# A streaming encoder step on one core: the four slots of the weights' upper halves begin at four residues modulo 256 bytes instead of one

## The chip, the core and the metric

The kernel runs on one core of a Trainium2 chip. The metric is the device time of one execution, in microseconds (us), lower is better.

## The reference, cut to what matters

Two layers over 320 tokens (256 of a prompt, 64 of a decoding step), model width 2048, all in float32:

```
h = rms_norm(x, g_mix)
aq, ak, av, bq, ... , dfl = split(h @ w_in)          # w_in: 2048 x 4392
o = concat(attention A, B, C, D)                      # four kinds of attention
x = x + o @ w_out                                     # 2048 x 2048
x = x + square(relu(rms_norm(x, g_mlp) @ w_up)) @ w_down   # 2048 x 8192, 8192 x 2048
x = x + (ple @ w_ple) * sigmoid(rms_norm(x, g_ple) @ w_ple_gate)
```

The outputs are the activations and the new rows of the caches.

## The kernel before, in words

**Weights in a ring.** All weights stream from HBM through `ring`, four slots of 1024 float32 in each of 128 partitions (4096 bytes a slot). One slot's fill is a unit, 512 KB; unit n goes to slot n modulo 4. There are 408 units a layer: 108 in a first part (w_in, the small projections of C, and part of w_out) and 300 in the tail (the last quarter of w_out 8, the MLP 256, w_ple 4, w_ple_gate 32). SyncE issues the loads (L464).

**Two halves.** The products keep float32 precision by splitting. ACT writes the upper half of a unit, rounded to the format fp32r, to the slot of the same number in `whi` (L1125 in the first part, L1141 in the tail). POOL subtracts it from the ring and writes the lower half, in four pieces of 256 columns: in the first part into the ring itself under the name `rlo` (L655), in the tail into `wlo` (L669). TensorE then makes three products, lower half of the weights by upper half of the activations, upper by lower, and upper by upper.

**w_in** (`w_in_piece`, L767, L769, L770): the activations (`xw`, `xv`) are stationary, loaded as 128x128 blocks, and the weights move, 256 to 512 columns at a time. For two of the three tiles of tokens there are three products, rlo, whi, whi; for the third two, rlo, whi. These pieces are woven into the attention by hand written lists (`FILL`, `AT`), so that TensorE has work while ACT and DVE do softmax.

**The tail** (`gemm_chunk`, `tail_unit`, `product`; L706, L707, L708): here the weights are stationary and the activations move, 320 columns at a time. A unit is two blocks of 128 rows by 512 columns: for each of 4 column blocks m and 2 row blocks k come wlo with the upper activations (L706), whi with the lower (L707), whi with the upper (L708), 24 matmuls. Four PSUM banks take a chunk of eight units, and the other four are emptied by DVE meanwhile. The MLP is four times 32 units of w_up and 32 of w_down.

**Waits.** TensorE waits for `lo_ready` (POOL's lower half of the unit), POOL for `hi_ready` (ACT), ACT for `raw_loaded` (the DMA) and for `unit_used` (TensorE has done with the unit four before). A load in the tail waits for `lo_ready` of the unit four before.

**Where things lie.** Addresses in SBUF come from `sb`, one after another, or are given. The offset of a partition's byte modulo 256 is called the residue here. Steps from block to block and from slot to slot are multiples of 256 bytes in the tail, so a tile keeps its residue throughout (512 bytes from m to m, 2048 from k to k in the weights, 1280 from block to block in the activations). Residues before:

| operand | role | residue |
|---|---|---|
| `whi`, `wlo`, `ring`, `rlo` | all four slots | 128 |
| `xw`, `xv` | stationary in w_in | 128 |
| `xhi`, `hhi` | moving, upper halves | 128 |
| `xlo` | moving, lower half of w_up and w_ple_gate | 192 |
| `hlo` | moving, lower half of w_down | 64 |
| `pleh`, `plel` | moving, both halves in w_ple | 160 |
| `hlast` | moving, lower half in the last of w_out | 160 |

`ahead` is a scratch tile of 3072 float32 that shares its place with `whi`, used while attention runs.

Of the kernel before, what the change touches and what calls it, by code (L numbers as in the profile page):

```python
# [24 lines left out]
UK = 2  # L25
XW = 256 + 128
RING = 4
# [35 lines left out]
def build(nc, I, O):  # L63
    f32 = mybir.dt.float32
    ALU, ACT, AX = mybir.AluOpType, mybir.ActivationFunctionType, mybir.AxisListType
    X = AX.X
    ctx = ExitStack()
    with ctx:
        f32r = mybir.dt.float32r
        top = [nc.sbuf_base + (-nc.sbuf_base) % 64]  # L70

        def sb(name, shape, dtype=f32, at=None):

            words = 1
            for n in shape[1:]:
                words *= n
            if at is None:
                at = top[0]
                top[0] += 4 * (words + (-words) % 8)
            return nc.alloc_sbuf_tensor_at(name, shape, dtype, offset=at)  # L80

        def sem(name):
            return ctx.enter_context(nc.semaphore(name))

        at = top[0]
# [16 lines left out]
        wlo = sb("wlo", [128, RING, 1024], f32r, top[0] - 4 * RING * 1024)  # L102
        at = top[0]
# [8 lines left out]
        at = top[0]  # L112
        ring = sb("ring", [128, RING, 1024])
        rlo = sb("rlo", [128, RING, 1024], f32r, at)
        at = top[0]
        whi = sb("whi", [128, RING, 1024], f32r)
        ahead = sb("ahead", [128, 3072], at=at)
        table = sb("table", [128, T_END])
        vec = sb("vec", [128, VW])
# [3 lines left out]
        at = top[0]  # L123
# [22 lines left out]
        at = top[0]  # L146
# [41 lines left out]
        hi_ready = sem("hi_ready")  # L188
# [173 lines left out]
        for j in ORDER:  # L362
            PREP_BASE[j] = tuple(_t)
            n = len(PREP[j])
# [320 lines left out]
        def _(pe):  # L685
            mm = nc.tensor.matmul

            def hold(s, value):

                pe.wait_ge(s, value)  # L690
                pe.sem_inc(pe_passed, 1)
# [6 lines left out]
            def tail_unit(l, q4, u):  # L698

                hold(lo_ready, l * HL + N_WU + 4 * q4 + u + 1 - TAIL0)  # L700
                return [w[:, u % RING, :].rearrange("p (a n) -> p a n", a=UK) for w in (whi, wlo)]

            def product(out, w, k, m, x2, start, stop):

# [5 lines left out]
            def gemm_chunk(l, q4, half, chunk_no, src, before_unit=None, before_last=None, units=KB // UK, first=0):  # L710


                nk = UK
                hold(half_free, l * CHUNKS + chunk_no + 1)
                for u in range(units):
                    w = tail_unit(l, q4, first + u)
                    if before_unit:
                        before_unit(u)
                    for m in range(4):
                        if m == 3 and u == 0 and before_last:  # L720
                            before_last()
                        for k in range(nk):
                            last = product(ps[:, 4 * half + m, 0:TOK], w, k, m, src(u * nk + k),
                                           u == 0 and k == 0, u == units - 1 and k == nk - 1)
                        if u == units - 1 and m < 3:
                            last.then_inc(bank_full, 1)
                    last.then_inc(unit_used, 1)
# [264 lines left out]
            with pe.Fori(0, DEPTH) as l:  # L992
# [55 lines left out]
                for c in range(4):  # L1048
                    hold(half_free, l * CHUNKS + 36 + c + 1)
                    w = tail_unit(l, Q_PLE, c)  # L1050
                    for m in range(4):
                        for k in range(2):
                            last = product(ps[:, 4 * (c % 2) + m, 0:TOK], w, k, m, (pleh[:, k, :], plel[:, k, :]),
                                           k == 0, k == 1)
                        last.then_inc(bank_full if m < 3 else unit_used, 1)
# [9 lines left out]
            for i in range(12):  # L1065
# [3 lines left out]
                n = 128 if t < 2 else DSEQ  # L1069
# [45 lines left out]
        def _(act):  # L1115
            A = nc.scalar.activation
# [19 lines left out]
            def upper_halves(l, n, slots=range(RING)):  # L1136

                for s in slots:
                    act.wait_ge(raw_loaded[s], 16 * (l * SLOT + n + 1))
                    act.wait_ge(unit_used, l * UNITS + RING * n + s + 1)  # L1140
                    A(whi[:, s, :], ring[:, s, :], ACT.Copy).then_inc(hi_ready, 1)  # L1141

            def x_uppers(p, b0):

# [86 lines left out]
            def attention(l, j):  # L1231
# [30 lines left out]
                if j == len(GROUPS) - 1:  # L1262
                    upper_halves(l, TAIL0 // RING, (0, 1))
# [6 lines left out]
            with act.Fori(0, DEPTH) as l:  # L1270
# [10 lines left out]
                for j, g in enumerate(GROUPS):  # L1281
# [17 lines left out]
                    attention(l, j)  # L1299

                upper_halves(l, TAIL0 // RING, (2, 3))
                for c in range(4):
                    upper_halves(l, TAIL0 // RING + 1 + c // 2, (2 * (c % 2), 2 * (c % 2) + 1))
                    act.wait_ge(half_free, l * CHUNKS + 2 + c + 1)
                    x_uppers(1, 4 * c)
                    if c < 3:
                        A(hid[:, 4 * c:4 * c + 4, :], x[:, 4 * c:4 * c + 4, :], ACT.Square).then_inc(mlp_squares, 1)
# [576 lines left out]
```

## Time and profile before

| | us |
|---|---|
| median of 3 runs | 3377.69 |
| lowest and highest | 3377.07, 3391.3 |
| the profiled execution's own time | 3379.88 |
| its span | 3378.1 |
| granted TensorE clock over the span | 0.99 |

The profile is of one execution. Busy time is per engine; loads of weights (PEld) run beside matmuls (PE). The tail of the first layer lies at 650 to 1696 us of the span, that of the second at 2316 to 3362. A matmul's duration in the trace goes from its start to its modelled end, and successive ones overlap; the distance between two starts is what each adds.

### The profile page before, as it was taken

The page shows a single profiled execution, that of the slowest core. Times are in us where ns is not written, and L with a number is a line of the kernel's source. Part 1 is how long each engine was busy: PE and PEld are TensorE (multiplying, and loading weights), DVE is VectorE, ACT ScalarE, POOL GpSimd, SP SyncE. Part 2 cuts the span into 40 slices and gives each one's busy share as a digit, 9 for nine tenths or more (in the row PEclk, how much of TensorE's full clock was granted, in tenths as well). Part 3 has the DMA queues.
Part 4 walks back from the last instruction along what each step waited for, and adds up shares of the span by engine and source line. Part 5 has one row for each costly group of instructions (what it writes and reads, how often), then busy time and mean ns, then how long its engine had stood idle before and what let it go on. Part 6 is the DMA issues. An engine that isn't in the chain of part 4 may idle for free.

```text
span 3378.1 us, 60314 instructions
## 1 busy us (share of the span) xinstructions
PE 3285.3 (97%) x20664; PEld 2977.2 (88%) x20664; DVE 1229.2 (36%) x2211; ACT 1138.0 (34%) x1666; POOL 2223.1 (66%) x2989
## 2 busy tenths in 40 slices
PE   7999999999999999999989999999999999999998
PEld 5777766799999999999977776668999999999998
DVE  4334564542041230323253445545411402304143
ACT  3333332433333333334343432424333333333342
POOL 4655200388898898888765551005888988889885
PEclk9999999999999999999999999999999999999999
DMA  5443322354454554544453433224545445455443
GB/s 153 134 123 111 111 73 83 100 152 152 151 151 155 150 152 154 150 154 151 133 157 114 129 93 112 71 84 124 149 151 155 150 151 155 150 152 154 150 145 123
DMA packets 295722, 453.02 MB, mean 134 GB/s; under 512 B 36336, under 2 KB 111344, under 8 KB 294832
## 3 DMA queue, kind: packets, MB, share of 16 engines
q1 hardware_dynamic: 295328, 448.66, 44.0%
q8 instruction: 176, 2.88, 0.3%
q14 instruction: 74, 0.61, 0.1%
q0 software_dynamic: 144, 0.87, 0.1%
HBM read 435.54 MB, written 14.06 MB: 133 GB/s over the span
## 4 chain that ended last, share of the span: by engine, by line
PE 91%; DVE 3%; issue 2%; DMA 1%; ACT 1%; SPq 1%; POOL 0%; DVEq 0%; ACTq 0%; POOLq 0%
PE ps L707 21%; PE ps L708 21%; PE ps L706 20%; PE ps L804 5%; PE ps L792 5%; PE ps L767 5%; PE ps L770 4%; PE ps L769 3%; PE ps L896 2%; DMA ring<-in_w_in 1%; PE ps L931 1%; PE ps L842 1%; PE ps L900 1%; PE ps L899 1%; PE ps L865 1%
## 5 line engine op out<-in xcount | busy, mean ns | idle before, releaser
L669 POOL TENSOR_TENSOR wlo<-ring,whi 128x256 fp32r<-128x256 f32 x2400 | 1803.5, 785 | 786.5 <-ACT whi L1141 786.0
L1141 ACT ACTIVATE whi<-ring 128x1024 fp32r<-128x1024 f32 x600 | 635.9, 1061 | 1350.3 <-PE ps L708 1341.6
L707 PE MATMUL ps<-xlo,whi 128*128 128x320 f32 x2560 | 794.9, 311 | 0.0
L708 PE MATMUL ps<-xhi,whi 128*128 128x320 f32 x2560 | 788.0, 308 | 0.0
L706 PE MATMUL ps<-xhi,wlo 128*128 128x320 f32 x2560 | 781.7, 305 | 0.0
L708 PE MATMUL ps<-hhi,whi 128*128 128x320 f32 x2176 | 672.2, 309 | 0.0
L706 PE MATMUL ps<-hhi,wlo 128*128 128x320 f32 x2176 | 659.3, 303 | 0.0
L655 POOL TENSOR_TENSOR rlo<-ring,whi 128x256 fp32r<-128x256 f32 (+2 forms) x576 | 415.9, 755 | 325.4 <-ACT whi L1125 325.4
L707 PE MATMUL ps<-hlo,whi 128*128 128x320 f32 x2048 | 629.9, 308 | 0.0
L706 PEld LDWEIGHTS ps<-xhi,wlo 128*128 128x128 f32 x2560 | 483.8, 189 | 0.6
L708 PEld LDWEIGHTS ps<-xhi,whi 128*128 128x128 f32 x2560 | 480.6, 188 | 0.0
L707 PEld LDWEIGHTS ps<-xlo,whi 128*128 128x128 f32 x2560 | 480.2, 188 | 0.3
L706 PEld LDWEIGHTS ps<-hhi,wlo 128*128 128x128 f32 x2176 | 408.5, 188 | 0.1
L708 PEld LDWEIGHTS ps<-hhi,whi 128*128 128x128 f32 x2176 | 408.4, 188 | 0.0
L767 PE MATMUL ps<-rlo,xw 128*128 128x512 f32 (+3 forms) x1056 | 366.5, 353 | 32.9 <-DVE xw L1357 16.8
L1347 DVE TENSOR_TENSOR x<-ps,x 128x320 f32<-128x320 f32 x224 | 107.0, 488 | 781.4 <-PE ps L708 764.4
L707 PEld LDWEIGHTS ps<-hlo,whi 128*128 128x128 f32 x2048 | 383.0, 187 | 0.0
L770 PE MATMUL ps<-whi,xw 128*128 128x512 f32 (+3 forms) x1056 | 358.0, 345 | 0.0
L767 PEld LDWEIGHTS ps<-rlo,xw 128*128 128x128 f32 x1056 | 201.4, 191 | 65.3 <-issue 42.5
L1771 DVE SCALAR_TENSOR_TENSOR t<-ps,rfeat 128x320 f32<-128x320 f32 x128 | 61.6, 481 | 517.6 <-PE ps L708 517.4
L769 PE MATMUL ps<-whi,xv 128*128 128x512 f32 (+3 forms) x704 | 243.7, 346 | 0.0
L792 PE MATMUL ps<-hid,ring 128*128 128x320 f32 x768 | 225.3, 445 | 5.7 <-ACT vtok L1189 3.3
(244 smaller groups left out, 3160.7 us busy)
## 6 DMA issues: line engine op xcount, KB each, us to landing
ring<-in_w_up SPq DMA_DIRECT2D x256, 512.0 KB, 3.7
ring<-in_w_down SPq DMA_DIRECT2D x256, 512.0 KB, 3.6
ring<-in_w_in SPq DMA_DIRECT2D x120, 512.0 KB, 3.6
ring<-in_w_out SPq DMA_DIRECT2D x64, 512.0 KB, 4.0
ring<-in_w_ple_gate SPq DMA_DIRECT2D x64, 512.0 KB, 3.6
xsave<-x SPq DMA_DIRECT2D x8, 640.0 KB, 5.9
x<-xsave SPq DMA_DIRECT2D x8, 640.0 KB, 4.3
ring<-in_w_in SPq DMA_DIRECT2D x16, 288.0 KB, 2.9
```

The source lines that it names most:

```text
L655: last = nc.gpsimd.tensor_tensor(rlo[:, s, c:c + w], ring[:, s, c:c + w], whi[:, s, c:c + w].bitcast(f32), ALU.subtract)
L669: last = nc.gpsimd.tensor_tensor(wlo[:, s, c:c + LO_COLS], ring[:, s, c:c + LO_COLS], whi[:, s, c:c + LO_COLS].bitcast(f32), ALU.subtract)
L706: mm(out, lo[:, k, cols], xh, start=start, stop=False)
L707: mm(out, hi[:, k, cols], xl, start=False, stop=False)
L708: return mm(out, hi[:, k, cols], xh, start=False, stop=stop)
L767: mm(out, head, lo[:, k, :], start=(kk == 0), stop=False)
L769: mm(out, xv[:, kk, t * 128:(t + 1) * 128], hi[:, k, :], start=False, stop=False)
L770: last = mm(out, head, hi[:, k, :], start=False, stop=(kk == KB - 1))
L792: last = mm(ps[:, out_bank(r * KB + b), 0:TOK], w[:, k - k0, c:c + 128], hid[:, k, :], start=(k == k0), stop=(k == k1 - 1))
L804: return nc.tensor.transpose(out, in_, ident[0:in_.shape[0], 0:in_.shape[0]])
L1141: A(whi[:, s, :], ring[:, s, :], ACT.Copy).then_inc(hi_ready, 1)
L1347: return V.tensor_tensor(out, a, b, ALU.add)
```

## The change

`whi` gets 1040 columns a slot in place of 1024, of which the first 1024 are used. A slot is then 4160 bytes, so slots 0, 1, 2 and 3 begin at the residues 128, 192, 0 and 64. Nothing else about size or order changes; `table` and all tiles behind it lie 256 bytes further, at the same residues.

```diff
-        whi = sb("whi", [128, RING, 1024], f32r)
+        whi = sb("whi", [128, RING, 1024 + 16], f32r)
+        top[0] = at + 4 * RING * 1024 + 256
         ahead = sb("ahead", [128, 3072], at=at)
@@ tail_unit
-                return [w[:, u % RING, :].rearrange("p (a n) -> p a n", a=UK) for w in (whi, wlo)]
+                return [w[:, u % RING, 0:1024].rearrange("p (a n) -> p a n", a=UK) for w in (whi, wlo)]
@@ upper_halves
-                    A(whi[:, s, :], ring[:, s, :], ACT.Copy).then_inc(hi_ready, 1)
+                    A(whi[:, s, 0:1024], ring[:, s, :], ACT.Copy).then_inc(hi_ready, 1)
```

## Rows read from the trace of the kernel before

**Rows 1.** The page: span, busy time of each engine, granted clock in 40 slices.

```profile
span 3378.1 us, 60314 instructions
...
PE 3285.3 (97%) x20664; PEld 2977.2 (88%) x20664; DVE 1229.2 (36%) x2211; ACT 1138.0 (34%) x1666; POOL 2223.1 (66%) x2989
...
PEclk9999999999999999999999999999999999999999
```

**Rows 2.** The page: the chain that ended last, by engine and by line.

```profile
PE 91%; DVE 3%; issue 2%; DMA 1%; ACT 1%; SPq 1%; POOL 0%; DVEq 0%; ACTq 0%; POOLq 0%
PE ps L707 21%; PE ps L708 21%; PE ps L706 20%; PE ps L804 5%; PE ps L792 5%; PE ps L767 5%; PE ps L770 4%; PE ps L769 3%; PE ps L896 2%; DMA ring<-in_w_in 1%; PE ps L931 1%; PE ps L842 1%; PE ps L900 1%; PE ps L899 1%; PE ps L865 1%
```

**Rows 3.** The page's costliest groups (xcount | busy us, mean ns | idle before).

```profile
L707 PE MATMUL ps<-xlo,whi 128*128 128x320 f32 x2560 | 794.9, 311 | 0.0
L708 PE MATMUL ps<-xhi,whi 128*128 128x320 f32 x2560 | 788.0, 308 | 0.0
L706 PE MATMUL ps<-xhi,wlo 128*128 128x320 f32 x2560 | 781.7, 305 | 0.0
L708 PE MATMUL ps<-hhi,whi 128*128 128x320 f32 x2176 | 672.2, 309 | 0.0
L706 PE MATMUL ps<-hhi,wlo 128*128 128x320 f32 x2176 | 659.3, 303 | 0.0
...
L707 PE MATMUL ps<-hlo,whi 128*128 128x320 f32 x2048 | 629.9, 308 | 0.0
```

**Rows 4.** One line each of w_down, w_up, first w_up (ns min/median/max, first, last start).

```profile
L708 PE MATMUL ps<-hhi,whi x256: 309/309/310, 1014.4 to 1124.9; 128*128 128x320 f32 x128
...
L708 PE MATMUL ps<-xhi,whi x255: 307/307/308, 903.9 to 1013.9; 128*128 128x320 f32 x128
...
L706 PE MATMUL ps<-xhi,wlo x191: 307/308/385, 707.6 to 791.7; 128*128 128x320 f32 x191
```

**Rows 5.** Timeline of w_ple (start us, duration us, engine, line).

```profile
1568.74 0.31 PE L706 MATMUL ps<-pleh,wlo 128*128 128x320 f32 x1
1568.74 0.19 PEld L707 LDWEIGHTS ps<-plel,whi 128*128 128x128 f32 x1
...
1570.94 0.31 PE L706 MATMUL ps<-pleh,wlo 128*128 128x320 f32 x1
```

**Rows 6.** Timeline of PE in w_in, 512 columns.

```profile
44.73 0.39 PE L769 MATMUL ps<-whi,xv 128*128 128x512 f32 x1
...
50.85 0.39 PE L770 MATMUL ps<-whi,xw 128*128 128x512 f32 x1
...
57.36 0.63 PE L770 MATMUL ps<-whi,xw 128*128 128x512 f32 x1
...
59.07 0.63 PE L767 MATMUL ps<-rlo,xw 128*128 128x512 f32 x1
```

**Rows 7.** Windows (PE, PEld, DVE, ACT, POOL busy; granted clock; DMA share, GB/s).

```profile
57.00:59.40 2.40, 2.40 (x7) 1.94 (x6) 0.00 (x0) 2.40 (x4) 2.40 (x4) 0.50 0.00 0
```

**Rows 8.** The tile whi: its instructions (ns min/median/max), what ACT waited for.

```profile
L707 PEld LDWEIGHTS ps<-xlo,whi x2560: 186/187/192, 678.9 to 3361.5; 128*128 128x128 f32 x197
...
L669 POOL TENSOR_TENSOR wlo<-ring,whi x2400: 720/742/1042, 646.4 to 3351.6; 128x256 fp32r<-128x256 f32 x185
...
L770 PE MATMUL ps<-whi,xw x1056: 274/389/632, 35.0 to 2056.6; 128*128 128x512 f32 x96, 128*128 128x256 f32 x48, 128*128 128x264 f32 x16, 128*128 128x288 f32 x16
...
L769 PE MATMUL ps<-whi,xv x704: 274/389/632, 34.6 to 2056.0; 128*128 128x512 f32 x96, 128*128 128x256 f32 x48, 128*128 128x264 f32 x16, 128*128 128x288 f32 x16
L1141 ACT ACTIVATE whi<-ring x600: 1037/1061/1066, 645.1 to 3348.0; 128x1024 fp32r<-128x1024 f32 x150
...
  PE ps L708: 1341.6, 560
```

**Rows 9.** POOL's group in the windows 2600 to 2700 and 2700 to 2800.

```profile
L669 POOL TENSOR_TENSOR wlo<-ring,whi 128x256 fp32r<-128x256 f32 x117 | 93.3, 832 | 7.7 <-ACT whi L1141 7.7
...
L669 POOL TENSOR_TENSOR wlo<-ring,whi 128x256 fp32r<-128x256 f32 x117 | 82.9, 739 | 18.4 <-ACT whi L1141 18.4
```

## The prediction

> **What bounds the kernel now.** I read the page first. TensorE is busy for 97% of the span, almost all of it at the full granted clock [rows 1], and the chain that ended last runs through PE for 91% [rows 2]. Three lines of that chain, L706 to L708, hold 62% of the span: the three products of every 128x128 weight block in the tail of each layer. No other engine is near: POOL 66%, DVE 36%, ACT 34% [rows 1]. So time comes or goes by how often TensorE can start a matmul, and the next view to read is that of the starts. The tail has 14400 matmuls of 320 columns: 2 layers, 300 units, 24 each. The five groups of the page with 2560 or 2176 of them, and that of 2048, hold 14080 [rows 3]; the rest are the first eight units and the four of w_ple.
>
> The page's mean of 303 to 311 ns is no price, because successive matmuls overlap. The price is the distance between starts. 320 columns at 2.4 GHz are 133.3 ns. What the rows show:
> - w_down in the middle of the MLP: the L708 starts of 256 triples run from 1014.4 to 1124.9, so 110.5 / (255 x 3) = **144.4 ns** a matmul. w_up before it: 110.0 / (254 x 3) = 144.4 [rows 4].
> - w_ple: the L706 at 1568.74 and the one at 1570.94 are 15 matmuls apart: **146.7 ns** [rows 5].
> - the first w_up block, after a wait at 707 us: 84.1 / (190 x 3) = **147.5 ns** until its end [rows 4]. Same code, same addresses as the 144.4 of the later w_up.
> - w_in, 512 columns: 28 starts from 44.73 to 50.85, 27 distances, give 226.7 ns against 213.3 ideal, so again 13.3 over. A few us later, from 57.36 to 59.07, four distances take 1.71 us [rows 6] at the granted clock 0.50, 1.2 GHz [rows 7]: 427.5 against 426.7 ideal, no excess at all.
>
> Each matmul thus pays 11 to 14 ns over its columns at 2.4 GHz and nothing at 1.2 GHz. What differs between the stretches is where operands begin modulo 256 bytes. In w_ple the moving operands begin at 160 in all three products, in w_in (512 and 256 columns) everything begins at 128: 13.3 ns over. In w_up they begin at 128, 192, 128, in w_down at 128, 64, 128: 11.1 ns over, that is 3 x 2.2 = 6.7 ns saved in every three. The 147.5 shows that it isn't addresses alone: a stream can also lock into a dearer rhythm and stay in it.
>
> **The change, part by part.** No instruction, wait or DMA is added or removed, and nothing is moved in any queue. The tiles behind whi move by exactly 256 bytes, so their residues stay; the third line (top) gives the same address as the allocation gives by itself. ahead keeps its place and length. What alters is the start of whi in slots 1, 2 and 3.
>
> (a) *whi as the moving operand*, w_in. L769 has 704 matmuls and L770 1056 [rows 8], so there are 704 triples rlo, whi, whi and 352 pairs rlo, whi. rlo stays at 128. In three slots of four the moving start now changes twice in a triple, just as in w_up. By that rhythm a triple saves 6.7 ns and a pair two thirds of it: (704 x 6.7 + 352 x 4.4) x 3/4 = 4.7 us. PE is the chain here too for most of the stage, so I count all of it. Bounds: 0 if changing starts pay only with 320 columns, and all the excess gone, 2816 matmuls x 13.3 x 3/4 = 28 us; on the other side the dearer rhythm of 0.8 ns more, 2 us lost. I take 4.7, the row nearest in form.
>
> (b) *whi as the stationary operand*, the tail. The load of the next weights starts with each matmul: L707's load at 1568.74, at the same time as the L706 matmul [rows 5]. Two reads of SBUF therefore run side by side, and the excess exists only at the clock at which they run fastest. No row has weights at another residue than 128, so this can't be read off. From both sides: w_ple, 160 against 128 throughout, costs the same 13.3 as w_in with 128 against 128. So a constant distance between the two reads is worth nothing; only its change within the triple was worth 6.7 ns. With the new starts the distances within a triple are, in w_up, (0, 64, 0), (-64, 0, 0), (128, 192, 0), (64, 128, 0) for the four slots, against (0, 64, 0) in all today; in w_down likewise two slots with one odd distance and two with three different ones. Nearest row for a triple with some change in it: 144.4, as now. I take **0 us** for (b). Ends: if three different distances save a second 6.7 ns in half of the units, 2400 triples x 6.7 = 16 us gained (all 11.1 ns of excess gone there would be 7200 x 11.1 = 80); if the units fall into the 147.5 rhythm, 3.0 ns each, 14400 x 3.0 = 43 us lost at most.
>
> The Trainium skill speaks against any effect of (b) ("TensorE: Matmul & The Clock Gate", Step-by-step): the engine has two independent read ports in SBUF, and loading the next weights doesn't steal bandwidth from the running matmul. By it (a) and (b) would both be 0 and the time 3377.7. The trace agrees at the low clock only; at the high one it shows 146.7, 144.4 and 147.5 for the same work.
>
> (c) *ACT and POOL on whi.* ACT writes it in 1061 ns, and its idle time of 1342 us is all waiting for PE; POOL reads it in a median of 742 ns [rows 8]. A unit takes PE 24 x 144.4 = 3.47 us, ACT 1.06 and POOL 4 x 0.74 = 2.97. Both hide behind PE, with three units of lead in the ring. Cover is thinnest at 2600 to 2700, where DVE shares the time: POOL busy 93.3 of 100, mean 832 ns, 7.7 idle [rows 9]. I count 0; if each POOL operation took over 8% longer, POOL would end last in such stretches.
>
> **Sum.** 4.7 + 0 + 0 = 4.7 us off. The profiled execution took 3379.9 us (span 3378.1), 2.2 above the median of 3377.7; its sum becomes 3375.2, and against the median the forecast is **3373 us**.
>
> **Rivals.**
> 1. *Weights' starts count, and pay.* Two reads side by side, excess only at full clock, and an excess that falls when the distance varies, all speak for it; that three kinds of shift were never seen together speaks against. 3377.7 - 16 - 4.7 = **3357 us**. Chance 0.33, a quarter of that for more than the 3350 below.
> 2. *Nothing depends on it.* The load of weights never meets the stream of the moving operand, and the 2.2 ns between 146.7 and 144.4 come from something else, or only with 320 columns. Both (a) and (b) are 0: **3377.7 us**, chance 0.11. Against it speaks that w_ple and w_up run the same three products of the same shape and differ; for stationary operands nothing speaks against it. This is what the Trainium skill's rule above would give.
> 3. *Slower: the dear rhythm becomes the usual one.* Its place is the tail. Today the change of slot after 24 matmuls alters nothing and a stream stays where it is, at 144.4 for 770 us of the first layer or at 147.5 after the wait at 707. With another distance in each slot the stream is pushed every 3.5 us and may lock in the dear rhythm. In the units of the three moved slots: 10800 x 3.0 = 32 us, less 4.7: **3405 us**. It decides (0.5% slower, 17 us) from (17 + 4.7) / 43 = half of the matmuls on. For it: one wait of PE was enough to bring the dear rhythm for 84 us. Against it: the w_down that followed went back to 144.4 by itself. Chance 0.20.
> 4. *POOL slows* by the 8% of (c) and more. Nothing shows its reads to depend on starts. 10% on 2400 operations of 742 ns is 178 us of POOL, nearly all hidden, some 20 us at most not. Chance 0.02.
>
> **How the numbers follow.** The measurement can tell about 0.5%, 17 us, from no change. The forecast has 0.34; with rival 2 that makes 0.45 within 0.5%. Faster is rival 1, 0.33; slower are rivals 3 and 4, 0.22. The range goes from 3350, below rival 1's own price, to 3403, short of rival 3's: 0.08 is left out below and 0.11 above. The forecast's own range is 3365 to 3380.
>
> **What would show it.** Same counts of instructions in every group. Step (a): in w_in the starts of 512 columns at 224 to 225 ns in units of slots 1 to 3, and 226.7 in slot 0. Step (b): 3.47 us from one unit to the next in the MLP for all four slots; a period of four units with different lengths would prove (b) wrong, shorter ones for rival 1 (3.41), longer for rival 3 (3.54). The stretch from the first matmul of w_up at 678.9 [rows 8] to w_ple at 1568.7 [rows 5] tells it by its length alone: 890 us now. (c): ACT 1061 ns and POOL 742 ns again, PE without idle time in the tail. The forecast is wrong if that length moves by more than 0.5%, whichever way.

## The result, and the profile after

The changed kernel is slower: median 3408.6 us (3405.0 to 3417.7) against 3378.3 us, ratio 1.0077 with a 95% interval of 1.0056 to 1.0098, that is 19 to 33 us. The forecast was 3373 with a range up to 3403, so the time lies outside; the price worked out for rival 3 was 3405.

The page of the changed kernel. Its lines are one higher than those of before from L117 on, so L707 to L709 are the L706 to L708 of before.

```profile
span 3403.2 us, 60314 instructions
...
PE 3313.1 (97%) x20664; PEld 3000.7 (88%) x20664; DVE 1226.3 (36%) x2211; ACT 1138.7 (33%) x1666; POOL 2221.4 (65%) x2989
...
L670 POOL TENSOR_TENSOR wlo<-ring,whi 128x256 fp32r<-128x256 f32 x2400 | 1801.8, 786 | 809.7 <-ACT whi L1142 809.4
L1142 ACT ACTIVATE whi<-ring 128x1024 fp32r<-128x1024 f32 x600 | 635.9, 1061 | 1374.6 <-PE ps L709 1364.7
```

The counts are the same, the span is 25.1 us longer, and PE has 27.8 us more busy time, while the busy times of ACT (1061 ns an operation) and POOL (median 740 ns) are as they were. So no other engine became the bound: TensorE itself starts its matmuls further apart. One line each of w_down and w_up, as in [rows 4]:

```profile
L709 PE MATMUL ps<-hhi,whi x256: 304/309/312, 1016.6 to 1128.6; 128*128 128x320 f32 x128
...
L709 PE MATMUL ps<-xhi,whi x256: 304/308/318, 903.8 to 1016.1; 128*128 128x320 f32 x128
```

w_down: 112.0 / (255 x 3) = 146.4 ns a matmul, w_up: 112.3 / (255 x 3) = 146.8 ns, both 144.4 before. From the start of the first matmul of w_up to that of w_ple it is 901.5 us in place of 889.9, in both layers: 2 x 11.6 = 23.3 of the 25.1 us. (The expectation of the first experiment has 11.8 and 23.6, read from starts in tenths of a microsecond.) The rest of the tail gives 1.0 us more, 24.3 us in all, so that 0.8 us is left for everything outside the tail.

Inside a block the four slots can be told apart by ACT, which starts on a slot as soon as TensorE has done with its unit. ACT's timeline in w_down (start, duration, idle before and what ended it), first of the kernel before, then of the changed one:

```profile
1062.81 1.06 ACT L1141 ACTIVATE whi<-ring 128x1024 fp32r<-128x1024 f32 x1 [2.41 <-PE ps L708]
1066.27 1.06 ACT L1141 ACTIVATE whi<-ring 128x1024 fp32r<-128x1024 f32 x1 [2.40 <-PE ps L708]
1069.74 1.06 ACT L1141 ACTIVATE whi<-ring 128x1024 fp32r<-128x1024 f32 x1 [2.41 <-PE ps L708]
```

```profile
1062.16 1.06 ACT L1142 ACTIVATE whi<-ring 128x1024 fp32r<-128x1024 f32 x1 [2.41 <-PE ps L709]
1065.70 1.06 ACT L1142 ACTIVATE whi<-ring 128x1024 fp32r<-128x1024 f32 x1 [2.49 <-PE ps L709]
1069.22 1.06 ACT L1142 ACTIVATE whi<-ring 128x1024 fp32r<-128x1024 f32 x1 [2.45 <-PE ps L709]
1072.74 1.06 ACT L1142 ACTIVATE whi<-ring 128x1024 fp32r<-128x1024 f32 x1 [2.46 <-PE ps L709]
1076.21 1.06 ACT L1142 ACTIVATE whi<-ring 128x1024 fp32r<-128x1024 f32 x1 [2.41 <-PE ps L709]
```

Before, every unit takes 3.47 us. After, the lengths are 3.54, 3.52, 3.52 and 3.47, and the same four come again: a period of four units, the sign that the prediction named for step (b) being wrong. The same from all 64 units of each kind (distance from a unit's first matmul to the next unit's, divided by its 24 matmuls; medians, ns a matmul):

| slot (residue of whi) | w_up before | w_up after | w_down before | w_down after |
|---|---|---|---|---|
| 0 (128) | 144.5 | 147.7 | 144.5 | 144.7 |
| 1 (192) | 144.5 | 147.3 | 144.5 | 147.8 |
| 2 (0) | 144.5 | 146.4 | 144.5 | 146.4 |
| 3 (64) | 144.5 | 146.1 | 144.5 | 146.7 |

Two things are in this table. Slots 1 to 3 are dearer in both blocks. And slot 0, where every operand lies as before, is dear in w_up as well, but hardly in w_down. A cell of the table stands for 64 units, 1536 matmuls. The means of slot 0 rose by 2.35 ns in w_up and 0.43 in w_down, which gives (2.35 + 0.43) x 1536 = 4.3 us; slots 1 to 3 give 19.0 us.

### The profile page after: what moved, and what is told of

Its sections match the earlier page's. It is cut to its first block, busy times and chain, and to the rows that moved or that the text cites. A ratio compares the mean times of both kernels' runs of the same rounds, so it can differ in the third digit from the quotient of the medians.

```text
span 3403.2 us, 60314 instructions
## 1 busy us (share of the span) xinstructions
PE 3313.1 (97%) x20664; PEld 3000.7 (88%) x20664; DVE 1226.3 (36%) x2211; ACT 1138.7 (33%) x1666; POOL 2221.4 (65%) x2989
## 4 chain that ended last, share of the span: by engine, by line
PE 91%; DVE 3%; issue 2%; DMA 1%; ACT 1%; SPq 0%; POOL 0%; DVEq 0%; ACTq 0%; POOLq 0%
PE ps L708 21%; PE ps L709 21%; PE ps L707 21%; PE ps L805 5%; PE ps L768 5%; PE ps L793 5%; PE ps L771 4%; PE ps L770 3%; PE ps L897 2%; PE ps L932 1%; DMA ring<-in_w_in 1%; PE ps L901 1%; PE ps L843 1%; PE ps L900 1%; PE ps L866 1%
## 5 line engine op out<-in xcount | busy, mean ns | idle before, releaser
L670 POOL TENSOR_TENSOR wlo<-ring,whi 128x256 fp32r<-128x256 f32 x2400 | 1801.8, 786 | 809.7 <-ACT whi L1142 809.4
L1142 ACT ACTIVATE whi<-ring 128x1024 fp32r<-128x1024 f32 x600 | 635.9, 1061 | 1374.6 <-PE ps L709 1364.7
L709 PE MATMUL ps<-xhi,whi 128*128 128x320 f32 x2560 | 792.1, 309 | 0.0
L708 PE MATMUL ps<-xlo,whi 128*128 128x320 f32 x2560 | 791.7, 309 | 0.0
L707 PE MATMUL ps<-xhi,wlo 128*128 128x320 f32 x2560 | 790.5, 309 | 0.0
L709 PE MATMUL ps<-hhi,whi 128*128 128x320 f32 x2176 | 671.0, 308 | 0.0
L707 PE MATMUL ps<-hhi,wlo 128*128 128x320 f32 x2176 | 669.2, 308 | 0.0
L708 PE MATMUL ps<-hlo,whi 128*128 128x320 f32 x2048 | 635.5, 310 | 0.0
L656 POOL TENSOR_TENSOR rlo<-ring,whi 128x256 fp32r<-128x256 f32 (+2 forms) x576 | 415.9, 756 | 328.2 <-ACT whi L1126 328.1
L707 PEld LDWEIGHTS ps<-xhi,wlo 128*128 128x128 f32 x2560 | 482.5, 188 | 0.6 <-issue 0.3
L708 PEld LDWEIGHTS ps<-xlo,whi 128*128 128x128 f32 x2560 | 481.1, 188 | 0.3
L709 PEld LDWEIGHTS ps<-xhi,whi 128*128 128x128 f32 x2560 | 480.7, 188 | 0.0
L707 PEld LDWEIGHTS ps<-hhi,wlo 128*128 128x128 f32 x2176 | 409.7, 188 | 0.1
L709 PEld LDWEIGHTS ps<-hhi,whi 128*128 128x128 f32 x2176 | 409.2, 188 | 0.0
L708 PEld LDWEIGHTS ps<-hlo,whi 128*128 128x128 f32 x2048 | 384.0, 188 | 0.0
```

The source lines that it names most:

```text
L656: last = nc.gpsimd.tensor_tensor(rlo[:, s, c:c + w], ring[:, s, c:c + w], whi[:, s, c:c + w].bitcast(f32), ALU.subtract)
L670: last = nc.gpsimd.tensor_tensor(wlo[:, s, c:c + LO_COLS], ring[:, s, c:c + LO_COLS], whi[:, s, c:c + LO_COLS].bitcast(f32), ALU.subtract)
L707: mm(out, lo[:, k, cols], xh, start=start, stop=False)
L708: mm(out, hi[:, k, cols], xl, start=False, stop=False)
L709: return mm(out, hi[:, k, cols], xh, start=False, stop=stop)
L1142: A(whi[:, s, 0:1024], ring[:, s, :], ACT.Copy).then_inc(hi_ready, 1)
```

## The experiments

The ratios are against the kernel before, timed in the same rounds; its median there was 3381 to 3386 us, so the times are not to be set beside the 3378.3 above. Executions of one kernel differ by 8 to 14 us, and the long ones have the lower mean granted clock (spans of the kernel before in one set of rounds: 3389.4 us at 0.985, 3377.4 at 0.990); in the traces of the kernel before and of the changed one the tail has the full clock throughout. So the readings below use the length of a block of the MLP (32 units, 768 matmuls), from its first matmul to the next block's. In the three kernels whose tail has the residues of before (the kernel before, the one with w_in alone and the one with a step of 256) it is the same within 0.05 us.

**The tail alone.** An edit of the changed kernel: w_in gets a name of its own for the upper halves, with all slots at 128.

```diff
+        whw = sb("whw", [128, RING, 1024], f32r, at)
-                hi, lo = (w[:, n % RING, 0:nk * ncol].rearrange("p (a n) -> p a n", a=nk) for w in (whi, rlo))
+                hi, lo = (w[:, n % RING, 0:nk * ncol].rearrange("p (a n) -> p a n", a=nk) for w in (whw, rlo))
```

(the write in L1126 and POOL's read in L656 likewise)

> Only the tail uses the shifted slots; w_in reads and writes the upper halves at residue 128 in all four slots, as before. The profile of the changed kernel is 25.1 us longer in its span, of which the stretch from the first w_up to w_ple gives 11.8 us in each layer, 23.6 in all. Theory A (the start of the stationary operand counts in the tail): that 23.6 us stays, the time is 3378 + 24 = 3402 us, and w_in with 512 columns is back at 226.7 ns a matmul. Theory B (the loss is made in w_in and only shows in the tail): near 3378 us and a unit of the MLP at 144.4 ns a matmul.

Measured: 3410.6 us against 3383.9, ratio 1.0077 (1.0055 to 1.0099), the blocks at 112.7 and 112.5 us as in the changed kernel, and w_in with 512 columns back at 226.7 ns in all slots. As far as the time can tell, the whole loss is in the tail's part.

**w_in alone.** The reverse, again from the changed kernel: the tail reads `wht`, with all slots at 128.

```diff
+        wht = sb("wht", [128, RING, 1024], f32r, at)
-                return [w[:, u % RING, 0:1024].rearrange("p (a n) -> p a n", a=UK) for w in (whi, wlo)]
+                return [w[:, u % RING, 0:1024].rearrange("p (a n) -> p a n", a=UK) for w in (wht, wlo)]
```

(ACT's write in L1142 and POOL's read in L670 likewise)

> Only w_in uses the shifted slots; the tail has residue 128 in all four. Theory A: the tail is back at 144.4 ns, and the time is 3378 us plus what w_in alone makes: by the matmuls with 512 columns, which went from 226.7 to between 229 and 237 ns in slots 1 to 3, some 1152 x 6 ns = 7 us if all of it lay on the path, less for the 256-column ones that went from 120 to 118; so 3378 to 3385. My prediction of a gain of 4.7 us would give 3373.

Measured: ratio 1.0012 (1.0002 to 1.0021), 1 to 7 us slower, blocks back at 110.9 us. So the forecast's only gain is a small loss.

**A step between slots without another residue.** From the changed kernel, with the tiles behind moved to match.

```diff
-        whi = sb("whi", [128, RING, 1024 + 16], f32r)
+        whi = sb("whi", [128, RING, 1024 + 64], f32r)
```

> The slots of the upper halves are 4352 bytes long, so each begins 256 bytes further than the next slot did before, and all four begin at residue 128. Theory A (residues modulo 256 count, nothing else): the same as before, 3378 us, 144.4 ns a matmul in the MLP in all slots. Theory C (another step than 4096 bytes between slots, or a larger period than 256 bytes, costs): slots 1 to 3 differ from slot 0, and the time goes to about 3400 us.

Measured: ratio 0.9994 (0.9984 to 1.0004), blocks 110.9 us, w_in at 226.7 ns in all slots. So the step between slots does not count by itself, and 256 bytes leave everything as it was.

**One residue for all four slots**, three kernels, each an edit of the kernel before: 192, 0 and 64. The diff is that of 192 (`at + 64`); the other two have `at + 128` and `at + 192`.

```diff
-        whi = sb("whi", [128, RING, 1024], f32r)
+        whi = sb("whi", [128, RING, 1024], f32r, at + 64)
+        top[0] = at + 4 * RING * 1024 + 256
```

> All four slots of the upper halves begin at residue 192, 64 bytes further than before, with the old step of 4096 bytes, so no unit differs from the next. In the changed kernel the units of slot 1 (192) took 147.8 ns a matmul in w_down and 147.3 in w_up. Theory A (each pair of residues has its own price): all slots cost that, the 30 whole blocks of the MLP take 113.3 us each in place of 110.9, and the time is 3378 + 16 x 2.3 + 4 = 3415 us or above. Rival theory D (what costs is the change from slot to slot, which knocks the stream out of its cheap rhythm): with constant starts the stream locks again and the time is 3378 us.

> All four slots of the upper halves begin at residue 0. In the changed kernel the units of slot 2 (0) took 146.35 ns in w_down and 146.4 in w_up. Theory A: all slots cost that, 112.4 us for a block of 32 units, 16 blocks x 1.5 = 24 us, 3402 us. Theory D: 3378 us.

> All four slots of the upper halves begin at residue 64. In the changed kernel the units of slot 3 (64) took 146.7 ns in w_down and 146.1 in w_up. Theory A: all slots cost that, 112.6 and 112.2 us a block, 16 x 1.5 = 24 us, 3402 us. Theory D: 3378 us.

Measured: ratios 1.0139 (1.0117 to 1.0161) at 192, 1.0098 (1.0081 to 1.0115) at 0, 1.0086 (1.0070 to 1.0103) at 64. The windows 920 to 1010 (w_up) and 1020 to 1120 (w_down) show PE busy throughout at the full clock, with fewer matmuls in the same time (PE busy (x), granted clock, DMA share, GB/s). Before:

```profile
920.00:1010.00 90.00, 90.00 (x625) 1.00 0.51 152
1020.00:1120.00 100.00, 100.00 (x695) 1.00 0.48 153
```

With all slots at 192:

```profile
920.00:1010.00 90.00, 90.00 (x611) 1.00 0.51 148
1020.00:1120.00 100.00, 100.00 (x678) 1.00 0.45 148
```

With all at 64:

```profile
920.00:1010.00 90.00, 90.00 (x617) 1.00 0.53 152
1020.00:1120.00 100.00, 100.00 (x684) 1.00 0.46 149
```

Nothing changes from slot to slot in these kernels, so a loss does not need the change; theory D falls as the explanation of the whole, theory A stands. Its numbers came in part. At 192 the blocks took 113.5 us where 113.3 was expected, at 64 they took 112.3 and 112.6. At 0, w_up took 146.7 ns a matmul and w_down 147.8, where 146.4 was expected in both. I read this as the price of a slot not being wholly its own: it seems to depend also on how the unit before leaves the stream. One block of w_up at 192 points the same way, with 112.6 us where the others have 113.5.

ACT writes `whi` and POOL reads it, so their accesses moved too, and they could be the ones that TensorE meets. The trace of the kernel with all slots at 64 speaks against that. Triples of matmuls in its w_down take 146.63 ns a matmul while POOL is busy throughout (1026 triples) and 146.64 while it is idle (168); for ACT it is 146.54 and 146.65, for DVE 146.70 and 146.66. The loss is there whether or not these engines work.

**Both halves shifted alike**, an edit of the changed kernel.

```diff
-        wlo = sb("wlo", [128, RING, 1024], f32r, top[0] - 4 * RING * 1024)
+        wlo = sb("wlo", [128, RING, 1024 + 16], f32r, top[0] - 4 * RING * 1024 - 256)
```

> The changed kernel, and the lower halves' slots shifted in the same way (128, 192, 0, 64), so that within a unit all loads of weights begin at one residue, which changes from unit to unit. Theory A1 (what costs is the load's start changing within the three products, wlo at 128 and whi elsewhere): back to 144.4 ns in all slots, 3378 us plus the few us of w_in. Theory A2 (what counts is the distance between the load's start and that of the moving operand beside it): still dear, about 3400. Theory D (change from unit to unit): still dear, about 3400, with slot 0 dear as well.

Measured: ratio 1.0098 (1.0081 to 1.0114), blocks 112.6 us (w_up) and 112.8 us (w_down). A1 falls: that all loads of a unit begin at one residue doesn't help. Slot 0 is dear here too, 147.1 ns in w_up and 145.5 in w_down; so the change from unit to unit has a part in it, though it is not needed for a loss.

**The lower half of the weights alone**, to 192 (the diff) and to 64 (`- 64` in place of `- 192`).

```diff
-        wlo = sb("wlo", [128, RING, 1024], f32r, top[0] - 4 * RING * 1024)
+        wlo = sb("wlo", [128, RING, 1024], f32r, top[0] - 4 * RING * 1024 - 192)
```

> Only the lower halves of the tail's weights move, to 192 in all four slots; the upper halves stay at 128. One of three loads then begins elsewhere, the one that runs beside the upper by upper product (moving operand at 128). Theory R: a new set of distances, no number known; every departure of the weights from 128 cost 1.2 to 3.3 ns a matmul so far, so 112 to 113.5 us a block and 3400 to 3415 us. Rival: the load of the lower half doesn't count, since its partner beside it is the same as ever; 110.9 us a block and 3380 us.

> Only the lower halves of the tail's weights move, to 64 in all four slots. Same theories as with 192: R 112 to 113.5 us a block and 3400 to 3415 us; the rival 110.9 us a block and 3380 us. If 64 and 192 differ, the sign of the distance counts, not only that there is one.

Measured: ratios 1.0046 (1.0030 to 1.0061) and 1.0076 (1.0058 to 1.0095). At 192 w_up takes 112.2 us and w_down 111.8, a little under the 112 to 113.5 expected. At 64 w_up takes 112.1, and w_down 112.1 in four of its eight blocks and 114.35 in the other four, with nothing between: two rhythms for one set of addresses. One displaced load of three is enough. The sign of the distance makes 0.2 ns a matmul in w_up, and in w_down 0.4 or 3.3 by the rhythm.

**The moving lower halves** at 0, with the weights as before.

```diff
-        xlo = sb("xlo", [128, KB, TOK], f32r, at + 4 * KB * TOK + 64)
+        xlo = sb("xlo", [128, KB, TOK], f32r, at + 4 * KB * TOK + 128)
-        hlo = sb("hlo", [128, KB, TOK], f32r, at)
+        hlo = sb("hlo", [128, KB, TOK], f32r, at + 192)
```

> The weights stay as before; the moving lower halves xlo and hlo go to residue 0, 128 bytes from everything else, in place of 192 and 64. Theory R with the distance's size mattering: a block could come out cheaper or dearer than 110.9 us, between 102.4 (no excess) and 113.5. Rival (any difference within the three moving operands is worth the same 6.7 ns, as 192, 64 and 160 were): 110.9 us a block and 3380 us.

Measured: ratio 1.0066 (1.0048 to 1.0085); all blocks but the first at 112.64 us, 146.7 ns a matmul, which is w_ple's value [rows 5]. The gain of 2.2 ns that 192 and 64 had is gone at 0.

**All operands of w_up shifted by 64**, an edit of the kernel before (the line that moves `top` left out here).

```diff
+        whi = sb("whi", [128, RING, 1024], f32r, at + 64)
+        wlo = sb("wlo", [128, RING, 1024], f32r, top[0] - 4 * RING * 1024 - 192)
+        xhi = sb("xhi", [128, KB, TOK], f32r, at + 64)
+        xlo = sb("xlo", [128, KB, TOK], f32r, at + 4 * KB * TOK + 128)
```

> Every operand of w_up and w_ple_gate lies 64 bytes further than in the kernel before: both halves of the weights at 192 in all slots, xhi at 192, xlo at 0. The distances between operands are those of the kernel before, the residues are not. w_down keeps hhi at 128 and hlo at 64, against weights now at 192. Theory R (only the distances between the operands count): w_up blocks after the first at 110.9 us, w_down, whose distances (-64, -128, -64) are those of no kernel so far, at 112 to 114; about 3395 to 3400 us in all. Theory S (128 is a good residue in itself): w_up is dear too, 112.5 us or more.

Measured: ratio 1.0093 (1.0076 to 1.0111), 26 to 38 us, well above the 17 to 22 us that theory R gave. w_down takes 112.6 us (one first block 113.5), within what was expected, so the excess is in w_up. The second and third blocks of w_up in the first layer:

```profile
920.00:1010.00 90.00, 90.00 (x625) 1.00 0.52 152
1140.00:1230.00 90.00, 90.00 (x612) 1.00 0.50 147
```

The first window has exactly the 625 matmuls of before (110.95 us for the block); the second has 612, and all later blocks take 113.21 us, 147.4 ns a matmul. The kernel before has the same two values: 144.4, and 147.4 in the units of its first block from 707 us on (the 147.5 of [rows 4]). w_ple_gate, whose operands are moved in the same way, shows the cheap one again. After a quarter of its units it too has the matmul of the norm between two of its own (L750; see step (c) below). It runs at 147.4 ns up to there, and at 144.4 behind:

```profile
1628.00:1702.00 74.00, 74.00 (x513) 1.00 0.43 134
```

74 us for 513 matmuls are 144.3 ns. In the kernel before, the stream goes from 144.4 to 147.4 at that very place. So moving everything together keeps both prices, which is theory R (under S neither the 625 nor the 513 could come), while R's forecast of the time failed, because it took the cheap rhythm for granted. The same addresses have two rhythms, and the same disturbance can lead from either into the other. That w_down now hands over a stream that ends up in the dear one is my reading of the order of the blocks, and not tested.

**xlo at 64, in the kernel before and in the changed one.**

```diff
-        xlo = sb("xlo", [128, KB, TOK], f32r, at + 4 * KB * TOK + 64)
+        xlo = sb("xlo", [128, KB, TOK], f32r, at + 4 * KB * TOK + 192)
```

> The kernel before with the lower half of the tail's activations (xlo) at residue 64 in place of 192, the residue that hlo has in w_down. Weights stay at 128. w_down finds the cheap rhythm by itself after each disturbance, while w_up stays at 147.4 ns after the wait at 707 us, and so does w_ple_gate. If that comes from 192 against 64, the first w_up and w_ple_gate go to 144.4 ns: 24 units x 24 x 3.0 ns = 1.7 us in each of four stretches, 6.9 us in all, 3371 us. If the dear rhythm there is a matter of the wait alone: 3378 us.

> The changed kernel with xlo at 64 in place of 192, so w_up has the residues of w_down. In the changed kernel the units of slot 0, whose operands all lie where they did, took 147.7 ns a matmul in w_up but 144.7 in w_down. Theory L (the change of slot pushes the stream, and only with the lower half at 64 does it fall back into the cheap rhythm by itself): slot 0 in w_up goes to 144.7 too, slots 1 to 3 to the 147.8, 146.4 and 146.7 of w_down, a block of w_up to 112.5 us. Rival (the dear slot 0 belongs to something else in w_up, such as its epilogue on DVE): slot 0 stays at 147.7.

Measured, in the kernel before: ratio 0.9996 (0.9987 to 1.0006). The first block of w_up falls from 113.3 to 111.7 us in both layers, as far as expected. The length of w_ple_gate stays at 113.0 us (113.05 before), so that half of the expectation failed. Two windows of it, before and behind the matmul of the norm, show that the equal length hides another rhythm. The kernel before:

```profile
1583.00:1605.00 22.00, 22.00 (x154) 1.00 0.47 153
1612.00:1692.00 80.00, 80.00 (x545) 1.00 0.42 132
```

With xlo at 64:

```profile
1583.00:1605.00 22.00, 22.00 (x152) 1.00 0.46 146
1612.00:1692.00 80.00, 80.00 (x548) 1.00 0.42 132
```

Unit by unit it is 144.4 ns and then 147.4 before, and 146.7 throughout with xlo at 64, the value of w_ple that runs ahead of it. In w_up the very same residues run at 144.4. So this set has a cheap and a dearer rhythm too, and does not always leave the dearer one; why it stays here isn't known. The 3 us gained in w_up can't be seen in the time.

In the changed kernel: ratio 1.0085 (1.0069 to 1.0102). ACT's timeline in w_up, changed kernel first, then with xlo at 64:

```profile
931.89 1.06 ACT L1142 ACTIVATE whi<-ring 128x1024 fp32r<-128x1024 f32 x1 [2.45 <-PE ps L709]
935.43 1.06 ACT L1142 ACTIVATE whi<-ring 128x1024 fp32r<-128x1024 f32 x1 [2.48 <-PE ps L709]
938.97 1.06 ACT L1142 ACTIVATE whi<-ring 128x1024 fp32r<-128x1024 f32 x1 [2.47 <-PE ps L709]
942.48 1.06 ACT L1142 ACTIVATE whi<-ring 128x1024 fp32r<-128x1024 f32 x1 [2.46 <-PE ps L709]
945.99 1.06 ACT L1142 ACTIVATE whi<-ring 128x1024 fp32r<-128x1024 f32 x1 [2.45 <-PE ps L709]
```

```profile
924.57 1.06 ACT L1142 ACTIVATE whi<-ring 128x1024 fp32r<-128x1024 f32 x1 [2.41 <-PE ps L709]
928.11 1.06 ACT L1142 ACTIVATE whi<-ring 128x1024 fp32r<-128x1024 f32 x1 [2.49 <-PE ps L709]
931.63 1.06 ACT L1142 ACTIVATE whi<-ring 128x1024 fp32r<-128x1024 f32 x1 [2.45 <-PE ps L709]
935.15 1.06 ACT L1142 ACTIVATE whi<-ring 128x1024 fp32r<-128x1024 f32 x1 [2.46 <-PE ps L709]
938.62 1.06 ACT L1142 ACTIVATE whi<-ring 128x1024 fp32r<-128x1024 f32 x1 [2.41 <-PE ps L709]
```

With xlo at 192 four units take 3.54, 3.54, 3.51, 3.51 and none is short. With 64 they take 3.54, 3.52, 3.52, 3.47, the same as in w_down: slot 0 is at 144.7 ns again, the others at 147.8, 146.4, 146.7, and the block at 112.43 us. Every number of theory L came, and the rival, w_up's epilogue on DVE, is out. So the dear slot 0 of w_up hangs on the slots before it and on the residue of the lower half. With 64 the stream is back at the cheap price within a unit of slot 0, with 192 it is not.

## Why the prediction was wrong

**What bounds the kernel** held: PE alone, at the spacing of its starts. Reading starts and not durations was right: the group of wlo with the upper activations in w_up has a mean duration of 309 ns against 305, while that of whi with the lower fell from 311 to 309. One count was loose, and nothing rests on it: the 320 matmuls missing from the 14080 are w_ple's 192 and one product of three in the first eight units, whose other two stand in the groups of 2176.

**Step (b)**, "I take 0 us", is the step that failed. It read from w_ple against w_in that a constant distance between the load and the stream "is worth nothing; only its change within the triple", and took 144.4 ns for any triple with some change in it. Both comparisons were too narrow: w_ple is 32 bytes off, and the two series that gave 144.4 both had the weights at 128 and the lower half 64 bytes from it. The lower halves at 0 show that a change within the triple is worth nothing by itself: 146.7 ns, with distances of 128 and 0. Slot 1 in w_down is (-64, -128, 0) by its distances, in w_up (-64, 0, 0), "one odd distance" like the cheap triple of before, and in both it is the dearest of the moved slots, 147.8 and 147.3 ns. Measured for (b): 24.3 us lost in the tail, 23.3 of it in the MLP, where 0 was taken and the ends were 16 gained and 43 lost. What the runs show in place of the step is that the start of the loaded weights against that of the moving operand has a price by itself, with all four slots alike too (1.8 to 3.3 ns a matmul at 64, 0 and 192). The end on the side of the loss held it; the value taken from "the nearest row" did not, since no row had other weights' residues than 128.

**Step (a)**, 4.7 us gained, has the wrong sign: 1 to 7 us lost with w_in alone, though the two profiled executions leave only 0.8 us for it and all else outside the tail. The kernel with all slots at 64 shows it in a series of 512 columns (PE's timeline, first and last of 18 successive starts):

```profile
43.61 0.40 PE L770 MATMUL ps<-whi,xv 128*128 128x512 f32 x1
...
47.61 0.40 PE L771 MATMUL ps<-whi,xw 128*128 128x512 f32 x1
```

4.00 us over 17 distances are 235.3 ns against 226.7 [rows 6]. Over all pieces the medians in the changed kernel are 226.7 in slot 0, and in slots 1, 2, 3: 233.0, 229.2 and 234.3 in the triples, 235.3, 229.3 and 237.7 in the pairs. With 256 columns it is the other way, from 120.0 ns to between 116 and 120. The bound of "the dearer rhythm of 0.8 ns" was far too small: up to 11 ns came.

**Step (c)** held: 1061 ns for ACT and 740 for POOL's median. PE has no idle time in the tail. It has none in the kernel before either: what the prediction calls the wait at 707 us is the matmul that sums the squares for the norm, two records in the trace, with PE busy all through:

```profile
706.44 0.31 PE L708 MATMUL ps<-xhi,whi 128*128 128x320 f32 x1
706.59 0.70 PE L750 MATMUL ps<-acc,ones 128*128 128x320 f32 x2
706.89 0.55 PE L706 MATMUL ps<-xhi,wlo 128*128 128x320 f32 x1
```

So it was not a pause that brought the dear rhythm of rival 3, but at most a foreign matmul in the stream.

**Rival 3** had the sign and nearly the price (3405), partly by a mechanism that the runs bear out: with the slots at four residues even slot 0 runs dear, 4.3 us. The larger part, 19 us, is something that no rival named: a price of the pair of residues, which stays when all slots are alike. Rival 1 had the right suspicion, that the weights' starts count, with the wrong sign. That rival 3's 3405 came so near is luck in part: it charged 32 us to the moved slots, which cost 19, charged nothing to slot 0, and took 4.7 off for w_in, which gained nothing. The chances of rivals 1 and 3 together were 0.53; the error was to make the case between them, an effect of exactly zero, the likeliest after arguing that two reads run side by side, and to let the range end 2 us short of rival 3's price.

**The low clock.** The rule of the Trainium skill that spoke against an effect ("TensorE: Matmul & The Clock Gate", "Step-by-step: what each phase is for": two independent read ports, the load doesn't steal bandwidth from the running matmul) would leave it without effect where the weights begin. At the full clock the runs differ from that: moving the weights of the tail cost 1.1 to 4.5 ns a matmul. The one series at the granted clock 0.50 that was read agrees with it. PE's timeline in w_in of the kernel with all slots at 192, where whi is the moving operand:

```profile
57.10 0.63 PE L770 MATMUL ps<-whi,xv 128*128 128x512 f32 x1
57.53 0.63 PE L771 MATMUL ps<-whi,xw 128*128 128x512 f32 x1
57.96 0.63 PE L768 MATMUL ps<-rlo,xw 128*128 128x512 f32 x1
58.38 0.63 PE L770 MATMUL ps<-whi,xv 128*128 128x512 f32 x1
58.81 0.63 PE L771 MATMUL ps<-whi,xw 128*128 128x512 f32 x1
```

1.71 us for four, 427.5 ns, as before the change [rows 6], and no excess over the columns.

What stays open is the cause beneath the starts: the runs vary starting places alone. A stream without loads of weights was not tried, so that the load and the moving operand are the two partners is argued from the effect of their starts, and not shown by taking one away.

## What to carry to other kernels

Where TensorE runs fp32r matmuls back to back at the full clock, the places in SBUF of both operands modulo 256 bytes may be a tuning knob; here it was worth up to 3% of the matmul time (144.4 to 148.9 ns with 320 columns). It works by sets: weights at 128 with the moving series 128, 192 or 64, 128 was the cheapest found, the same set moved by 64 bytes as a whole has the same two prices, and every other set that was tried cost more. Try such a shift on one whole tile and read the distance between starts of each unit, not the durations and not the time alone; a ring whose slots begin at different residues paid the price of the bad ones here, and in w_up made the good slot dear as well. When no row of a trace has varied a quantity, its effect isn't zero by that: the range must reach both ends.

## What the runs showed of the hardware that was not expected

- The same addresses, code and clock give two steady rhythms: 144.4 and 147.4 ns in w_up, and 145.9 and 148.9 in w_down with the lower halves of the weights at 64. Which of them a block has goes with what ran before it: at the norm's matmul in w_ple_gate the stream goes from 144.4 to 147.4 in the kernel before, and from 147.4 to 144.4 with all operands moved by 64.
- With the lower half of the moving operand at 64, the first w_up is back at 144.4 ns behind the norm's matmul, with 192 it stays at 147.4. In w_ple_gate the same 64 runs at 146.7 throughout.
- A shift of all operands by 64 bytes keeps both rhythms to within 0.1 ns; a step of 256 bytes changes nothing.
- The column count matters: whi as a moving operand at another residue than 128 costs 2.5 to 11 ns with 512 columns and gains up to 4 with 256.
- At the granted clock 0.50, in w_in with 512 columns, nothing of it shows: 427.5 ns with whi at 128 and at 192.
